# Moving 25 gathered context rows out of the second layer's attention: ten ahead of the layer, fifteen behind it

## What is computed

```python
def peer_block(hb, w_q, sub_keys, u_tab, v_tab):
    ...
    top_s, pos = lax.top_k(cand_s, PEER_TOPK)
    expert = jnp.take_along_axis(cand_i, pos, axis=-1)
    g = jax.nn.softmax(top_s, axis=-1)
    u = u_tab[expert]
    act = jax.nn.gelu(jnp.einsum('nhkd,nd->nhk', u, hb).astype(jnp.float32))
    w = (g * act).astype(hb.dtype)
    return jnp.einsum('nhk,nhkd->nd', w, v_tab[expert])

def first_block(x, ...):
    for l in range(DEPTH):
        ...                      # norm, projections, mlstm, moba, nsa
        x = x + jnp.einsum('bse,ed->bsd', mix, w_out[l])
        h = rmsnorm(x, norm_ffn[l])
        u = jnp.square(jax.nn.relu(jnp.einsum('bsd,df->bsf', h, w_ff1[l])))
        x = x + jnp.einsum('bsf,fd->bsd', u, w_ff2[l])
    return x
```

## Time and profile before

| | us |
|---|---|
| median of three timed runs | 3037.69 (3026.2 to 3040.97) |
| the profiled execution, timed | 3038.96 |
| its span, first to last instruction | 3037.1 |
| PE busy | 2518.2 (83%) |
| VectorE busy | 1967.6 (65%) |
| ScalarE busy | 480.1 (16%) |
| GpSimd busy | 1309.3 (43%) |
| mean DMA rate over the span | 344 GB/s |
| mean granted TensorE clock | 0.916 |

### The profile page before, as it was taken

How to read it: one execution, slowest core, us unless ns; L and a number is a source line. 1 busy time by engine, 2 the same in 40 slices (tenths; PEclk the granted TensorE clock), 3 DMA queues, 4 the chain that set the end, 5 groups by cost and what they waited for, 6 DMA issues and landing times.

```text
span 3037.1 us, 25923 instructions
## 1 busy us (share of the span) xinstructions
PE 2518.2 (83%) x8462; PEld 1374.0 (45%) x8462; DVE 1967.6 (65%) x4823; ACT 480.1 (16%) x1413; POOL 1309.3 (43%) x1072
## 2 busy tenths in 40 slices
PE   5789987899986899587878888877898797888777
PEld 2256645774545684233544344323345443343333
DVE  1338868789668866431367767767665676777775
ACT  1111121000112000001211111111122111111111
POOL 0000546564664675356335444434410354445442
PEclk8899987999996999788989999989999899999999
DMA  7739867998885999989599999999950999999997
GB/s 272 287 115 397 288 262 246 351 389 312 321 336 195 372 403 409 376 324 375 215 351 402 419 419 420 421 418 417 398 202 25 395 419 418 419 421 421 421 421 308
DMA packets 249162, 1046.30 MB, mean 345 GB/s; under 512 B 20278, under 2 KB 53126, under 8 KB 176964
## 3 DMA queue, kind: packets, MB, share of 16 engines
q0 software_dynamic: 147456, 805.37, 66.4%
q1 hardware_dynamic: 98048, 233.05, 20.6%
q10 hardware_dynamic: 3524, 6.22, 0.6%
HBM read 1040.80 MB, written 3.77 MB: 344 GB/s over the span
## 4 chain that ended last, share of the span: by engine, by line
DMA 24%; PE 22%; DVE 7%; POOL 2%; issue 2%; ACT 1%; DVEq 0%; POOLq 0%; ACTq 0%
PE psum L1819 12%; PE psum L173 6%; DMA sb_second_ring<-in_peer_uv,sb_second_scores 5%; DMA sb_beside_slots<-in_peer_uv,sb_second_scores 5%; DMA sb_second_aux<-in_peer_uv,sb_second_scores 4%; DMA sb_second_work<-in_peer_uv,sb_second_scores 4%; DMA sb_second_mod<-in_peer_uv,sb_second_scores 2%; DMA sb_second_ring<-in_peer_w_q 2%; PE psum L2112 2%; DMA sb_beside_slots<-in_peer_uv,sb_beside_small 2%; PE psum L1305 1%; POOL sb_beside_slots L1579 1%; PE psum L167 1%; DVE sb_second_scores L1498 1%; DVE sb_second_scores L1495 1%
## 5 line engine op out<-in xcount | busy, mean ns | idle before, releaser
L2152 POOL DMA_INDIRECT sb_beside_slots<-in_peer_uv,sb_beside_chosen x330 | 452.2, 1370 | 356.6 <-DVE sb_beside_slots L2048 159.2
L1819 PE MATMUL psum<-sb_beside_slots,sb_second_scores 128*128 128x512 f32 x660 | 328.6, 641 | 96.4 <-ACT sb_second_scores L1763 96.3
L1819 PE MATMUL psum<-sb_second_ring,sb_second_scores 128*128 128x512 f32 x600 | 287.9, 630 | 63.1 <-ACT sb_second_scores L1763 63.1
L2048 DVE SCALAR_TENSOR_TENSOR sb_beside_slots<-sb_beside_slots,sb_beside_H 128x1024 f32<-128x1024 f32 x228 | 272.8, 1221 | 98.9 <-DMA sb_beside_slots<-in_peer_uv,sb_beside_chosen 89.1
L1579 POOL DMA_INDIRECT sb_beside_slots<-in_peer_uv,sb_second_scores x165 | 194.2, 1177 | 312.8 <-PE psum L1819 258.4
L173 PE MATMUL psum<-sb_f_arena,sb_f_ring 128*128 128x256 f32 (+1 forms) x1344 | 299.9, 387 | 9.0 <-issue 5.2
L173 PEld LDWEIGHTS psum<-sb_f_arena,sb_f_ring 128*128 128x128 f32 (+1 forms) x1344 | 254.3, 190 | 54.2 <-issue 11.0
L1579 POOL DMA_INDIRECT sb_second_ring<-in_peer_uv,sb_second_scores x150 | 181.9, 1213 | 199.4 <-PE psum L1819 183.0
L1677 DVE SCALAR_TENSOR_TENSOR sb_beside_slots<-sb_beside_slots,sb_second_H 128x1024 f32<-128x1024 f32 x165 | 199.7, 1222 | 86.4 <-DMA sb_beside_slots<-in_peer_uv,sb_second_scores 85.3
L1819 PEld LDWEIGHTS psum<-sb_beside_slots,sb_second_scores 128*128 128x128 f32 x660 | 132.0, 205 | 271.5 <-issue 148.6
L1677 DVE SCALAR_TENSOR_TENSOR sb_second_ring<-sb_second_ring,sb_second_H 128x1024 f32<-128x1024 f32 x150 | 181.0, 1223 | 76.9 <-DMA sb_second_ring<-in_peer_uv,sb_second_scores 76.9
(11 more groups left out here) (526 smaller groups left out, 3883.7 us busy)
## 6 DMA issues: line engine op xcount, KB each, us to landing
sb_f_ring<-in_w_ff SPq DMA_DIRECT2D x32, 2048.0 KB, 14.8
sb_context_ring<-in_ada_w SPq DMA_DIRECT2D x23, 2048.0 KB, 11.0
sb_f_ring<-in_w_in SPq DMA_DIRECT2D x8, 2048.0 KB, 13.5
sb_second_ring<-in_peer_w_q SPq DMA_DIRECT2D x16, 1024.0 KB, 25.5
sb_second_ring<-in_w_qkv SPq DMA_DIRECT2D x6, 2048.0 KB, 22.8
sb_f_ring<-in_w_in SPq DMA_DIRECT2D x6, 1904.0 KB, 14.9
sb_context_ring<-in_peer_w_q SPq DMA_DIRECT2D x8, 1024.0 KB, 10.2
sb_f_ring<-in_w_out SPq DMA_DIRECT2D x4, 2048.0 KB, 9.0
```

The lines of the kernel that those rows point to most:

```text
L1819: done = e.matmul(st.pair(("acc", g))[:, half, :], diag[:, n % (4 * BATCH), :], v_of(n)[:, half * 512:(half + 1) * 512], start=(f == 0 and ...
L2048: e.scalar_tensor_tensor(out=row, in0=row, scalar=1.0, in1=self.H[:, t, :], op0=ALU.mult, op1=ALU.mult, accum_out=self.dots[t][:, s:s + 1] ...
L2152: e.indirect_dma_start(out=self.slot(i), out_offset=None, in_=self.table, in_offset=bass.IndirectOffsetOnAxis(ap=at, axis=0), element_offs ...
```

## The change

In `vector` of `first_block`, every `rows_beside(1, 1)` and `rows_beside(2, 2)` amid the attention becomes `rows_beside(1, 0)` and `rows_beside(2, 0)`: 17 calls that held 25 steps in each layer now hold none in the second. In the second layer each of the eight feed-forward steps has 12 rows in place of 10. At the end of the first layer the last call has 19 in place of 9. All rows are still gathered and used, in the same order; the leftover call (L2811) takes the rest.

```diff
@@ -2692,7 +2692,7 @@
         e.tensor_reduce(hid, st.pair("cmps")[:, 0, 0:2 * P].rearrange("p (c g n) -> p c n g", c=2, g=4)[:, :, 0:NC_CMP, :], AX, ALU.add).then_inc(*st.empties("cmps"))
-        rows_beside(1, 1)
+        rows_beside(1, 0)
         e.wait_ge(sg_ready, 1)
...
@@ -2715,19 +2715,19 @@
         heads_out(0)
-        rows_beside(2, 2)
+        rows_beside(2, 0)
         scores(2)
-        rows_beside(1, 1)
+        rows_beside(1, 0)
...
@@ -2798,7 +2798,7 @@
         for c in range(8):
             routes = not last and c % 2 == 1
-            beside.vector(e, 10 if last else 6 if routes else 8)
+            beside.vector(e, 12 if last else 6 if routes else 8)
             e.wait_ge(*st.emptied(("ff1", c)))
@@ -2819,7 +2819,7 @@
                 beside.vector(e, 6)
                 routed_later(q)
-            beside.vector(e, 9)
+            beside.vector(e, 19)
             beside.mark_vector((l + 1, 0))
```

## The result

The median of 17 timed runs is 3046.82 us (3041.21 to 3054.98), that of the kernel before, timed beside it, 3036.29 (3026.2 to 3045.24): a ratio of 1.0034, 95% interval 1.0025 to 1.0043. The forecast was 3043 us, with a range of 3022 to 3057 and 0.70 for a difference under 0.5%. So the changed kernel takes 10.5 us more by the medians. The profiled execution of the changed kernel spans 3047.3 us, against 3037.1: +10.2. The forecast's sum was +5.5.

A forecast was written before the change was run, and what follows sets the result against it. VectorE's order was taken to bound the second layer's attention, transfers the stretch from about 1000 us; -16 + 2 + 19.5 = +5.5 us gave 3043 us after adjusting to the runs' median, range 3022 to 3057.

The forecast's parts named there:

- What bounds: Second layer: VectorE's order bounds the attention; transfers bound from about 1000 us to the end of the dot products.
- the signs: Trace marks of a right forecast, such as output projection 11 to 22 us earlier, dot products' end moved by 5 us.
- The attention: Second layer's attention without its 25 rows: 16 us saved, bounds 13.4 and 24.4.
- the lower bound: Attention's smaller saving, 13.4 us, from stepping the engines through their orders with PE's traced durations kept.
- The ten early rows: Ten rows moved to the end of the first layer: cost 2 us, bounds 0 and 8.8.
- uncovered: First layer's end: GpSimd's ten extra gathers ahead of its power step cost nothing; if not hidden, 1 to 3 us.
- The fifteen rows behind: Fifteen more rows behind the attention, where transfers are full: cost 19.5 us, bounds 18.7 and 23.
- PE untouched: Second layer's feed-forward: PE not delayed at first; late squares would be covered by 11.94 and 19.5 us of slack.
- Behind that end nothing changes: After the context's dot products: transposed weights, barrier and second half are released by that end, difference 0.
- Rival 1: Fuller steps from 1000 us on cost nothing, since slots limit there, not bytes: 3024 us, or 3016; chance 0.14.
- Rival 2: The ten early rows find no free transfer time and delay the second layer's masks: 3055 us; chance 0.16.
- Rival 3: PE and ScalarE bind the attention, so nothing is saved there: +21.5 us, 3059 us; chance 0.04.

The follow-up runs named there:

- e11: The changed kernel itself, run and profiled once more with nothing altered; ratio 1.0021 to the kernel before.
- e2: The changed kernel with 9 rows in place of 19 at the end of the first layer; ratio 1.0067 to the kernel before, 3055.0 us.
- e4: The changed kernel with the last 30 `u` gathers at half width; ratio 1.0011 to the kernel before.
- e1: The kernel before with 19 rows in place of 9 at the end of the first layer, nothing else; ratio 0.9968 to the kernel before, 3026.37 us.
- e5: The changed kernel with `u` gathers 158 to 187, amid the feed-forward, at half width; ratio 1.0002 to the kernel before.
- e6: The kernel before with 19 rows ending the first layer and 14 of the attention's 25 rows kept, placed in VectorE's waits; ratio 0.9978 to the kernel before.
- e8: The changed kernel with 22 more transposes on PE ahead of five waits in the second layer's attention; ratio 1.0021 to the kernel before.
- e10: As e9, with 22 more transposes on PE in the second layer's attention; ratio 0.9948 to the kernel before.
- e12: As e10, with SyncE's load of the experts' sub-keys moved ahead of the feed-forward's last weights; ratio 0.9954 to the kernel before, 3021.1 us.
- e9: As e6, with one more row per first-layer feed-forward step and the layer-end mark six rows ahead of its last row; ratio 0.9962 to the kernel before.

## Why the prediction came out right, and where its steps were off

**What bounds.** Right: the transfers from 1000 us on (1.03 in every row), and PE waiting behind them (forecast about 31 us of idle, measured 33.08 and 32.41). Of the signs, the end of the dot products was to move by 5 us and moved by 13.1 (10.0 in e11), and the projection was to come 11 to 22 us earlier and came 8.2 (11.1).

**The attention.** This is the term that was mis-sized: -16 taken, with bounds 13.4 and 24.4; -10.1 and -12.4 in the two profiles of the changed kernel, outside both bounds. The steps were right in place: the wait ahead of the compressed output (7.9 forecast, 9.4 measured), then the fourth and fifth outputs (3 and 1.8; 3.5 and 2.1). PE did idle less, as said. What failed is the conclusion that it would then run no slower than before: the lower bound kept the durations of before, as if a clock could only gain. From the masks to the projection the clock was 0.68 in the changed kernel and 0.70 before, and the same products took PE 70.24 us in place of 66.61. These 3.6 us are about what is missing from the 13.4. L3029 alone took 1.7 us longer on the path. In e2 and e4, at 0.73, the term was -15.5, near the value taken: so it is a matter of the clock in the run, not of the order. What sets the clock of a run is open.

**The ten early rows.** Right: masks +1.91 and +1.3 (changed, e11), and e1 with the part alone at -0.8. GpSimd's last gather ahead of its power step began at 774.88 and the step at 775.88, as worked out, at no cost. It is narrow, though: with 34 rows there, or eight more upstream, the same mechanism costs 14 to 30 us of idle PE. The prediction priced the seam at 1 to 3 us "uncovered", and that would have been far too little.

**The fifteen rows behind.** 19.5 forecast, 21.2 measured, within 18.7 to 23. A part of the excess may be a queue that must be filled from empty, which no run tests: in the first five microseconds of the projection (980 to 985 us) the share was 0.40, where the kernel before had 0.82 (985 to 990).
The page "DMA: Bandwidth & Descriptors" of the Trainium skill, section Specifications, puts HBM's limit per core near 358 GB/s. It did not bind this core: the changed kernel moved 399 and 407 GB/s in the two stretches from 1027.6 to 1253.8 us.

**PE untouched.** Nearly: the fifth square came at 1129.69 (1136.6 forecast), the eighth at 1200.72 (1207 forecast), and the accumulator's ReLU late by 1.56 us, ahead of L3063. PE's slack hid it, as said.

**Behind that end nothing changes.** Off by 2.9 us, to the good side. 1.4 of it is the barrier: it followed the last weights by 12.6 us before and by 11.2 in the changed kernel, in e2, e5, e6, e8 and e11. It is the landing of GpSimd's last gather, which took 9.8 us from its issue before and 8.5 in the changed kernel. The prediction had no term for it. The 1.5 us of the second half isn't explained.

**The rivals.** Rival 1, steps that cost nothing: fell by e1 and e2, 1.26 to 1.42 us a row. Rival 2, the debt: fell for ten rows (masks at +1.9); 25 rows do make one, but by GpSimd's order and not by the transfers that the rival named. Rival 3, nothing saved: fell, 10 to 15.5 us were. The range held, but not because every term did. The saving in the attention lay outside its own bounds by 3.3 us (1.0 in e11). The errors were 5.9 us in the attention and 1.7 behind it, and 2.9 us that were not forecast went the other way, which is luck. The range was wide enough for the rest by what the other terms and the rivals had put into it. The absolute 3043 us lies nearer to 3046.8 than the difference does (+5.5 forecast, +10.5 measured), because the kernel before, timed beside it, read 1.4 us less than in its first three runs.

**A version under both kernels.** e1, one number changed, is under both (0.9968), and e10 and e12 are the lowest (0.9948 and 0.9954); their intervals overlap with e1's.

## What to carry to other kernels

Work that hides behind transfers should be moved to where the transfers are idle, not to where the engine is: here each row costs 1.2 us of VectorE in the attention and 1.3 to 1.4 us of transfers behind it, so taking all of them out of a stretch with room for both loses. Rows that fill waits cost nothing there (e6's attention, 92.8 us with 14 rows), so they can stay; that such an order is faster than e1, which only moved ten rows ahead, isn't shown. And whatever is issued in order ahead of a small step that another engine needs (here GpSimd's power step behind the gathers) has to be counted as that step's delay.

## What the runs showed of the hardware

- TensorE's granted clock in one and the same order of short products, from the masks to the projection: 0.67 to 0.73 in six profiles, the stretch 94.1 to 88.6 us long. With 22 transposes in the waits it was 0.82, the stretch 84.0 us.
- Half-width gathers (2 KB for each of 128 tokens in place of 4) were not twice as quick: GpSimd, at 8.2 to 8.7 us of 10 in five to seven issues, had no time left.
- The issue of a small load (64 or 128 KB) held SyncE's queue for 18.3 to 19.5 us, whichever load stood at that place, with the transfers at a share of 1.03 (e9, 1207 to 1226 us).
- A gather of 128 rows of 4 KB took 6.7 to 14.7 us from its issue to its landing when it was the last ahead of the barrier, and the barrier came 1.6 to 1.7 us behind it in all fourteen profiles.
